# High and low words of a weight tile stored by turns, and weight loads with a stride of two words

## The chip, the cores and the metric

The kernel runs on one core of one Trainium2 chip. The metric is the device time in microseconds (us). Two runs of the kernel before took 2203.51 and 2210.92 us, a median of 2207.22 us.

## What the reference computes

Two stacks of transformer-like blocks work on one sequence: 16 meta tokens and 256 tokens, 1024 features. The first stack has two layers, each a feed-forward part, a mixer (stick-breaking attention beside a convolution of 31 taps) and a second feed-forward part. The second has two layers with differential attention in one and retention in the other, each again between two feed-forward parts. All of it is float32. Nearly all arithmetic is in products of the activations with large weight matrices, of which this is the typical one (2816 hidden features):

```
def swiglu(x, w_gate, w_up, w_down):
    return (jax.nn.silu(x @ w_gate) * (x @ w_up)) @ w_down

for l in range(DEPTH):
    h = h + 0.5 * swiglu(rmsnorm(h, ffn1_norm[l]), ffn1_w_gate[l], ffn1_w_up[l], ffn1_w_down[l])
    h = h + hybrid_mixer(rmsnorm(h, mix_norm[l]), ...)
    h = h + 0.5 * swiglu(rmsnorm(h, ffn2_norm[l]), ffn2_w_gate[l], ffn2_w_up[l], ffn2_w_down[l])
```

## The kernel before, in words

Activations lie with features on the 128 partitions and tokens along the free axis. A **phase** y is one feed-forward part, one mixer, the norm between the stacks, the differential attention or the retention; there are 13, numbered 0 to 12 in the list `PHASES`. Phases 0 to 4 work on all 272 tokens, the later ones on 256 (a mixer's second half already on the narrower set where the next phase is narrow).

**Weights.** SyncE streams 680 panels from memory, each 8 weight tiles of 128x128 (`K8`, 1024 words in a partition) or 11 of them (`K11`, 1408 words), into a ring of four slots, `raw`. TensorE multiplies in a reduced float32 format, so each operand is split into a high part and the rest. For each panel ScalarE writes the rounded high part (`act_split`, L405: `whi` from `raw`), and VectorE the remainder (`dve_split`, L412: `wlo` = `raw` - `whi`). `whi` and `wlo` are two rings of the same form as `raw`, and in each a weight tile is 128 words without a gap.

**Products.** Three matmuls are made for each weight tile k: high weights by high activations, high weights by low activations, low weights by high activations. That is `products` (L387, L388, L389), and `split_products` (L395, L396, L397) where the second goes to another half of the bank. Each matmul comes with a load of its weight tile, 128 words in each partition; the load for the next matmul runs while the present one streams its 272 or 256 activation columns.

**Activations.** The moving operands are in `u` (8 tiles high, 8 tiles low; the input of gate and up or of a mixer's projections), `hid` (22 and 22 tiles; the input of the down projection), in `qk`, `ao_hi` and `ao_lo` (mixers), and in `ry` (retention). `tile_of` gives the address of one: tile k of part 0 (high) or 1 (low), tiles 272 or 256 words apart. In the wide phases the first tile starts at the tensor's start; in the narrow ones it starts `U_PAD` = 112 or `HID_PAD` = 24 words later; `RY_PAD` does the same for `ry`.

**Distances.** With the tensors laid out in the order of the code, each at a multiple of 32 bytes, the start of the moving tile less the start of the weight tile that is loaded beside it comes, modulo 64 words, to this: 48 words in all narrow feed-forward, attention and retention steps; 0, 16, 32 and 48 words by turns in wide steps from `u`; 8, 24, 40 and 56 words by turns in wide steps from `hid` (a moving tile is 272 words further on, a weight tile 128). Within a step the distance is not constant: the moving stream goes through 256 or 272 words while the load goes through 128.

In four panels of eight of each retention head, and in one panel of three of differential attention, the weights are the moving operand and the activations are loaded (L940 to L943, L1049 to L1051).

**Order.** It is written out by hand. SyncE refills a slot of `raw` when VectorE has made the low part; ScalarE writes a slot of `whi` when TensorE has used the panel that was there (`panel_used`); TensorE waits for `lo_ready` at each panel's start, and for a free bank. Between the splits ScalarE and VectorE empty the banks: gates, products with the norm, and the splits of `hid` and `u`.

Of the kernel before, what the change touches and what calls it, by code (L numbers as in the profile page):

```python
# [18 lines left out]
RING = 4  # L19
# [53 lines left out]
def first_col(y):  # L73

    return 0 if y <= LAST_MIX else META
# [68 lines left out]
U_PAD, HID_PAD, RY_PAD = 112, 24, 144  # L144


def build(nc, w8, w11, xT, small, cst, lam, outT):
# [7 lines left out]
    with ctx:  # L155
# [8 lines left out]
        whi = sb("whi", [128, RING, K11], f32r)  # L164
        wlo = sb("wlo", [128, RING, K11], f32r)
# [3 lines left out]
        u = sb("u", [128, 2 * KD * T], f32r)  # L169
# [35 lines left out]
        with ExitStack() as area:  # L205
            hid = sb("hid", [128, 2 * FT * T], f32r, area)
# [158 lines left out]
        def tile_of(buf, tiles, pad, y, part, k, c0, c1):  # L365

            width, first, at = (T, 0, 0) if y <= LAST_MIX else (SEQ, META, pad)
            at += part * tiles * width
            parts = buf[:, at:at + tiles * width].rearrange("p (k c) -> p k c", c=width)
            return parts[:, k, c0 - first:c1 - first]  # L370

        def u_at(y, part, k, c0=None, c1=T):
            return tile_of(u, KD, U_PAD, y, part, k, first_col(y) if c0 is None else c0, c1)

        def hid_at(y, part, f):
            return tile_of(hid, FT, HID_PAD, y, part, f, first_col(y), T)
# [6 lines left out]
        def products(pe, out, slot, k, x_hi, x_lo, first, last):  # L383


            w_h, w_l = whi[:, slot, k * 128:k * 128 + 128], wlo[:, slot, k * 128:k * 128 + 128]
# [4 lines left out]
        def split_products(pe, out, slot, k, x_hi, x_lo, first, last):  # L391


            w_h, w_l = whi[:, slot, k * 128:k * 128 + 128], wlo[:, slot, k * 128:k * 128 + 128]
# [4 lines left out]
        def act_split(act, n, it=0):  # L399

            if not isinstance(it, int) or n < PANELS:
# [211 lines left out]
        def _(pe):  # L613
            def ffn(y):
# [4 lines left out]
                def gate_up(it, norm=False):  # L619

                    for j in range(RING):
# [4 lines left out]
                        for k in range(KD):  # L626
# [5 lines left out]
                            if N == SEQ:  # L632
                                mm = split_products(pe, bank[g % 4], n % RING, k, u_at(uy, 0, k),
                                                 u_at(uy, 1, k), k == 0, k == KD - 1)
                            else:
                                mm = products(pe, bank[g % 4][:, 0:N], n % RING, k, u_at(uy, 0, k),
# [13 lines left out]
            def out_proj(y, n0, per_tile, tiles, x, ready, count, N, lag=3):  # L650
# [4 lines left out]
                def tile(j, it, both):  # L655
                    pe.wait_ge(h_done, KD * (y + 1) + j - 1 + group * it)
                    for q in range(per_tile):
                        n = n0 + per_tile * j + q
                        pe.wait_ge(lo_ready, n + 1 + RING * it)
                        for k in range(tiles):  # L660
# [3 lines left out]
                            if both:  # L664
                                mm = split_products(pe, bank[4 + j % 2], n % RING, k, x(0, K), x(1, K), K == 0, K == last)
# [1685 lines left out]
```

## Time and profile before

| | |
|---|---|
| median of the runs | 2207.22 us |
| the profiled execution: its own time | 2210.91 us |
| its span, first to last instruction | 2209.1 us |
| TensorE matmul busy | 2198.0 us, 18114 matmuls |
| VectorE busy | 1602.4 us |
| ScalarE busy | 1276.6 us |
| GpSimd busy | 282.1 us |
| read from memory | 384.18 MB |

Matmuls are pipelined: each has a duration of about 280 ns in the profile, but the next starts some 115 to 126 ns after it. So what a matmul costs is not its duration but the distance between starts, and that is read by dividing a stretch in which TensorE is never idle by its number of matmuls. Below this is called a **step**.

### The profile page before, as it was taken

The page shows a single profiled execution, that of the slowest core. Times are in us where ns is not written, and L with a number is a line of the kernel's source. Part 1 is how long each engine was busy: PE and PEld are TensorE (multiplying, and loading weights), DVE is VectorE, ACT ScalarE, POOL GpSimd, SP SyncE. Part 2 cuts the span into 40 slices and gives each one's busy share as a digit, 9 for nine tenths or more (in the row PEclk, how much of TensorE's full clock was granted, in tenths as well). Part 3 has the DMA queues.
Part 4 walks back from the last instruction along what each step waited for, and adds up shares of the span by engine and source line. Part 5 has one row for each costly group of instructions (what it writes and reads, how often), then busy time and mean ns, then how long its engine had stood idle before and what let it go on. Part 6 is the DMA issues. An engine that isn't in the chain of part 4 may idle for free.

```text
span 2209.1 us, 48942 instructions
## 1 busy us (share of the span) xinstructions
PE 2198.0 (99%) x18114; PEld 2180.8 (99%) x18114; DVE 1602.4 (73%) x2450; ACT 1276.6 (58%) x1988; POOL 282.1 (13%) x328
## 2 busy tenths in 40 slices
PE   8999999999999999999999999999999999999999
PEld 8999999999999999999999999999999999999999
DVE  6655997665566579887768767888768766777775
ACT  6444786544444368766546646876556645565662
POOL 0001661100100136220020012010010010101000
PEclk9999999999999999999999999999999999999999
DMA  6555435555455544455555555355556645445553
GB/s 229 174 188 165 159 122 170 167 171 195 155 173 183 179 161 144 144 185 186 190 169 193 195 183 163 124 178 194 195 181 200 219 162 177 161 162 194 188 200 124
DMA packets 100408, 386.68 MB, mean 175 GB/s; under 512 B 11312, under 2 KB 12464, under 8 KB 100304
## 3 DMA queue, kind: packets, MB, share of 16 engines
q1 hardware_dynamic: 99648, 383.89, 52.2%
q8 instruction: 68, 1.11, 0.2%
q0 software_dynamic: 368, 1.26, 0.2%
q14 instruction: 36, 0.29, 0.0%
q10 hardware_dynamic: 288, 0.12, 0.0%
HBM read 384.18 MB, written 1.05 MB: 174 GB/s over the span
## 4 chain that ended last, share of the span: by engine, by line
PE 98%; ACT 1%; DVE 1%; issue 0%; DMA 0%; ACTq 0%
PE bank L387 16%; PE bank L389 15%; PE bank L388 15%; PE bank L395 15%; PE bank L396 14%; PE bank L397 14%; PE bank L759 1%; PE bank L1049 1%; PE bank L1050 1%; PE bank L1051 1%; PE bank L1096 0%; PE bank L709 0%; PE bank L740 0%; PE bank L940 0%; PE bank L943 0%; PE bank L942 0%
## 5 line engine op out<-in xcount | busy, mean ns | idle before, releaser
L412 DVE TENSOR_TENSOR wlo<-raw,whi 128x1024 fp32r<-128x1024 f32 (+1 forms) x677 | 893.3, 1322 | 177.8 <-ACT whi L405 165.4
L405 ACT ACTIVATE whi<-raw 128x1024 fp32r<-128x1024 f32 (+1 forms) x677 | 745.5, 1112 | 164.5 <-PE bank L389 117.2
L387 PE MATMUL bank<-u,whi 128*128 128x272 f32 (+1 forms) x1888 | 549.0, 291 | 7.1 <-DVE u L450 7.1
L389 PE MATMUL bank<-u,wlo 128*128 128x272 f32 (+1 forms) x1888 | 543.7, 288 | 0.0
L388 PE MATMUL bank<-u,whi 128*128 128x272 f32 (+1 forms) x1888 | 541.9, 287 | 0.0
L395 PE MATMUL bank<-u,whi 128*128 128x256 f32 x1888 | 529.2, 280 | 0.2
L397 PE MATMUL bank<-u,wlo 128*128 128x256 f32 x1888 | 527.4, 279 | 0.0
L396 PE MATMUL bank<-u,whi 128*128 128x256 f32 x1888 | 527.4, 279 | 0.0
L387 PEld LDWEIGHTS bank<-u,whi 128*128 128x128 f32 x1888 | 356.9, 189 | 8.0 <-DVE wlo L412 7.3
L388 PEld LDWEIGHTS bank<-u,whi 128*128 128x128 f32 x1888 | 357.0, 189 | 0.9 <-issue 0.2
L397 PEld LDWEIGHTS bank<-u,wlo 128*128 128x128 f32 x1888 | 357.6, 189 | 0.0
L395 PEld LDWEIGHTS bank<-u,whi 128*128 128x128 f32 x1888 | 356.4, 189 | 1.0 <-DVE wlo L412 0.5
L389 PEld LDWEIGHTS bank<-u,wlo 128*128 128x128 f32 x1888 | 356.7, 189 | 0.0
L396 PEld LDWEIGHTS bank<-u,whi 128*128 128x128 f32 x1888 | 354.6, 188 | 0.2
L397 PE MATMUL bank<-hid,wlo 128*128 128x256 f32 x770 | 215.0, 279 | 0.0
L395 PE MATMUL bank<-hid,whi 128*128 128x256 f32 x770 | 215.0, 279 | 0.0
L396 PE MATMUL bank<-hid,whi 128*128 128x256 f32 x770 | 215.0, 279 | 0.0
L437 ACT ACTIVATE u<-h,gain 128x256 fp32r<-128x256 f32 (+1 forms) x88 | 44.1, 512 | 280.6 <-DVE h L1650 136.9
L389 PE MATMUL bank<-hid,wlo 128*128 128x272 f32 (+1 forms) x638 | 183.2, 287 | 0.0
L387 PE MATMUL bank<-hid,whi 128*128 128x272 f32 (+1 forms) x638 | 182.9, 287 | 0.0
L388 PE MATMUL bank<-hid,whi 128*128 128x272 f32 (+1 forms) x638 | 182.3, 286 | 0.0
L397 PEld LDWEIGHTS bank<-hid,wlo 128*128 128x128 f32 x770 | 145.9, 190 | 0.0
(332 smaller groups left out, 3448.8 us busy)
## 6 DMA issues: line engine op xcount, KB each, us to landing
raw<-w SPq DMA_DIRECT2D x552, 512.0 KB, 3.4
raw<-w SPq DMA_DIRECT2D x128, 704.0 KB, 4.1
h<-xT SPq DMA_DIRECT2D x4, 272.0 KB, 4.9
outT<-h SPq DMA_DIRECT2D x8, 128.0 KB, 4.7
consts<-cst POOLq DMA_DIRECT2D x1, 576.0 KB, 4.6
dist<-cst POOLq DMA_DIRECT2D x1, 192.0 KB, 2.7
rdist<-cst POOLq DMA_DIRECT2D x1, 192.0 KB, 3.0
sgain<-small POOLq DMA_DIRECT2D x1, 145.5 KB, 4.8
```

The costliest lines, as they stand in the source:

```text
L387: pe.matmul(out, w_h, x_hi, start=first, stop=False)
L388: pe.matmul(out, w_h, x_lo, start=False, stop=False)
L389: return pe.matmul(out, w_l, x_hi, start=False, stop=last)
L395: pe.matmul(out[:, 0:SEQ], w_h, x_hi, start=first, stop=False, skip_group_check=True)
L396: pe.matmul(out[:, SEQ:2 * SEQ], w_h, x_lo, start=False, stop=last, skip_group_check=True)
L397: return pe.matmul(out[:, 0:SEQ], w_l, x_hi, start=False, stop=last, skip_group_check=True)
L405: act.activation(whi[:, n % RING, 0:COLS[n]], raw[:, n % RING, 0:COLS[n]], ACT.Copy).then_inc(hi_ready, 1)
L412: dve.tensor_tensor(wlo[:, n % RING, 0:COLS[n]], raw[:, n % RING, 0:COLS[n]], whi[:, n % RING, 0:COLS[n]], ALU.subtract).then_inc(lo_ready, 1)
L437: act.activation(u_at(y, 0, f), h[:, f, win(y)], ACT.Copy, scale=norm_gain(y, f)).then_inc(u_hi_ready, 1)
L759: mm = pe.matmul(bank[5][:, s0:T], vv[:, i, cols], at[:, hd % 2, c0:c0 + w], start=(i == 0 and n == 0), stop=(i == 2 and n == 2), skip_gro ...
L1049: pe.matmul(bank[2 + i][:, :], u_at(y, 0, k, tok.start, tok.stop), w_h, start=(k == 0), stop=False)
L1050: pe.matmul(bank[2 + i][:, :], u_at(y, 1, k, tok.start, tok.stop), w_h, start=False, stop=False)
```

## The change

The two rings `whi` and `wlo` become one, `whl`, with slots of 2816 words. In it, high and low words of a weight tile stand by turns: word 2c of a tile is the high part of column c, word 2c+1 its low part. `weights(part, n)` gives the view of a panel, [tile, column] with a stride of two words between columns, and ScalarE and VectorE write through this view, VectorE also reads the high part through it. A weight tile then takes 256 words. In the wide phases tiles of the 8-tile panels are laid 272 words apart (`GAP_STEP` = 136 pairs), as the moving tiles are. Panels in which the weights are the moving operand (`STREAMED`) stay as they were, high parts first, low parts after, without stride.

`U_PAD` and `HID_PAD` go. `U_PLACE` and `HID_PLACE` give for each phase the words by which the high tiles are set off from the tensor's start, and the further words by which the low tiles are set off. The tiles of `hid` are 320 words apart in the wide phases. `u` and `hid` become larger by 104 words, and by 2208. `whl` and `u` start at the same place modulo 64 words, and `hid` now too. The numbers in the two tables are therefore the distances, modulo 64 words, between the start of the moving tile and the start of a high weight tile; where a load is of the next tile in a wide 8-tile panel, it is 16 words less. Since the moving stream passes 256 words in the time in which a load passes 128 columns, now 256 words, the distance stays what it is through the whole load.

No instruction is added, removed or moved; splits have the form 128x8x128 in place of 128x1024, and loads a stride of two.

```
-U_PAD, HID_PAD, RY_PAD = 112, 24, 144
+RY_PAD, GAP_STEP, HID_STEP = 40, 136, 320
+U_PLACE = {0: (48, 0), 1: (32, 0), 2: (16, 0), 3: (0, 0), 4: (48, 32), 5: (48, 0), 6: (32, 0), 8: (48, 0), 9: (16, 0), 10: (0, 0), 11: (48, 0), 12: (48, 32), 7: (32, 0)}
+HID_PLACE = {0: (48, 0), 2: (32, 0), 3: (16, 0), 5: (32, 32), 7: (16, 32), 9: (48, 48), 10: (32, 16), 12: (32, 48)}
...
-        whi = sb("whi", [128, RING, K11], f32r)
-        wlo = sb("wlo", [128, RING, K11], f32r)
+        whl = sb("whl", [128, RING, 2 * K11], f32r)
...
-        u = sb("u", [128, 2 * KD * T], f32r)
+        u = sb("u", [128, 2 * KD * T + 104], f32r)
...
-            hid = sb("hid", [128, 2 * FT * T], f32r, area)
+            hid = sb("hid", [128, 2 * FT * HID_STEP + 96], f32r, area)
...
-            width, first, at = (T, 0, 0) if y <= LAST_MIX else (SEQ, META, pad)
-            at += part * tiles * width
-            parts = buf[:, at:at + tiles * width].rearrange("p (k c) -> p k c", c=width)
+            first = first_col(y)
+            at = part * tiles * step + sum(place[:part + 1])
+            parts = buf[:, at:at + tiles * step].rearrange("p (k c) -> p k c", c=step)
             return parts[:, k, c0 - first:c1 - first]
...
+        def weights(part, n):
+            tiles = COLS[n] // 128
+            if n in STREAMED:
+                return whl[:, n % RING, part * K8:part * K8 + K8].rearrange("p (k c) -> p k c", c=128)
+            step = GAP_STEP if n < BASE[LAST_MIX + 1]["P"] and COLS[n] == K8 else 128
+            return whl[:, n % RING, 0:2 * tiles * step].rearrange("p (k c i) -> p k c i", c=step, i=2)[:, :, 0:128, part]
...
-            w_h, w_l = whi[:, slot, k * 128:k * 128 + 128], wlo[:, slot, k * 128:k * 128 + 128]
+            w_h, w_l = weights(0, n)[:, k, :], weights(1, n)[:, k, :]
             pe.matmul(out, w_h, x_hi, start=first, stop=False)
             pe.matmul(out, w_h, x_lo, start=False, stop=False)
             return pe.matmul(out, w_l, x_hi, start=False, stop=last)
...
-                act.activation(whi[:, n % RING, 0:COLS[n]], raw[:, n % RING, 0:COLS[n]],
+                act.activation(weights(0, n), raw[:, n % RING, 0:COLS[n]].rearrange("p (k c) -> p k c", c=128),
                                ACT.Copy).then_inc(hi_ready, 1)
...
-                dve.tensor_tensor(wlo[:, n % RING, 0:COLS[n]], raw[:, n % RING, 0:COLS[n]],
-                                  whi[:, n % RING, 0:COLS[n]], ALU.subtract).then_inc(lo_ready, 1)
+                dve.tensor_tensor(weights(1, n), raw[:, n % RING, 0:COLS[n]].rearrange("p (k c) -> p k c", c=128),
+                                  weights(0, n), ALU.subtract).then_inc(lo_ready, 1)
...
-                        w_h, w_l = (w[:, n % RING, 512 * kk:512 * kk + 512] for w in (whi, wlo))
+                        w_h, w_l = (whl[:, n % RING, K8 * i + 512 * kk:K8 * i + 512 * kk + 512] for i in range(2))
```

## Rows read from the trace of the kernel before

**Rows 1.** Page, part 1: busy time, share of span, instructions.
```profile
PE 2198.0 (99%) x18114; PEld 2180.8 (99%) x18114; DVE 1602.4 (73%) x2450; ACT 1276.6 (58%) x1988; POOL 282.1 (13%) x328
```

**Rows 2.** Waits of TensorE: who waited for whom, us, times, longest.
```profile
PE bank L387 <- DVE u L450: 7.1, 1, 7.1
PE bank L909 <- DVE dn_lo L1966: 0.4, 1, 0.4
```

**Rows 3.** Windows: stretch, length, then busy us (instructions) by engine, clock, DMA share.
```profile
core 0: us, PE busy (x) PEld busy (x) DVE busy (x) ACT busy (x) POOL busy (x), PEclk, DMA share, GB/s
30.00:150.00 120.00, 120.00 (x954) 120.00 (x953) 76.19 (x118) 56.97 (x78) 0.00 (x0) 1.00 0.57 188
520.00:570.00 50.00, 50.00 (x401) 50.00 (x400) 25.57 (x29) 19.27 (x21) 6.30 (x9) 1.00 0.53 175
980.00:1070.00 90.00, 90.00 (x766) 90.00 (x766) 71.35 (x113) 55.61 (x96) 0.00 (x0) 1.00 0.56 187
1450.00:1800.00 350.00, 349.91 (x3080) 349.22 (x3079) 271.24 (x400) 208.37 (x330) 21.75 (x31) 1.00 0.59 195
2030.00:2120.00 90.00, 90.00 (x766) 90.00 (x766) 72.65 (x117) 56.77 (x98) 0.00 (x0) 1.00 0.57 192
830.00:960.00 130.00, 129.84 (x1104) 128.76 (x1103) 118.10 (x198) 103.14 (x182) 56.59 (x59) 1.00 0.45 151
```

**Rows 4.** Groups by line and form: first matmul of each three.
```profile
L395 PE MATMUL bank<-u,whi 128*128 128x256 f32 x1888 | 529.2, 280 | 0.2
L387 PE MATMUL bank<-u,whi 128*128 128x272 f32 x1504 | 439.3, 292 | 7.1 <-DVE u L450 7.1
L395 PE MATMUL bank<-hid,whi 128*128 128x256 f32 x770 | 215.0, 279 | 0.0
L387 PE MATMUL bank<-hid,whi 128*128 128x272 f32 x528 | 152.2, 288 | 0.0
L387 PE MATMUL bank<-u,whi 128*128 128x256 f32 x384 | 109.7, 286 | 0.0
```

**Rows 5.** Timeline of TensorE, wide phase: start, duration.
```profile
502.21 0.29 PE L387 MATMUL bank<-u,whi 128*128 128x272 f32 x1
502.35 0.28 PE L388 MATMUL bank<-u,whi 128*128 128x272 f32 x1
502.46 0.29 PE L389 MATMUL bank<-u,wlo 128*128 128x272 f32 x1
502.59 0.29 PE L387 MATMUL bank<-u,whi 128*128 128x272 f32 x1
```

**Rows 6.** Timeline of TensorE, narrow phase.
```profile
1499.94 0.28 PE L395 MATMUL bank<-u,whi 128*128 128x256 f32 x1
1500.05 0.28 PE L396 MATMUL bank<-u,whi 128*128 128x256 f32 x1
1500.16 0.28 PE L397 MATMUL bank<-u,wlo 128*128 128x256 f32 x1
```

**Rows 7.** Groups by line and form: splits, and VectorE for comparison.
```profile
L412 DVE TENSOR_TENSOR wlo<-raw,whi 128x1024 fp32r<-128x1024 f32 x549 | 686.2, 1252 | 92.5 <-ACT whi L405 80.3
L405 ACT ACTIVATE whi<-raw 128x1024 fp32r<-128x1024 f32 x549 | 574.7, 1052 | 133.1 <-PE bank L389 115.4 <-PE bank L1051 15.4 <-DMA raw<-w 1.8
L1694 DVE TENSOR_TENSOR pr<-sl,up 128x256 f32<-128x256 f32 x110 | 46.8, 426 | 4.7
L1637 DVE TENSOR_REDUCE gt<-bank 128x256 f32<-128x512 f32 x35 | 24.2, 692 | 50.7 <-PE bank L397 50.7
```

More of the change, by code:

```diff
@@ L141 @@
 DA_PANELS = [(part, n) for part, n in DA_PANELS if 0 <= n < DA_HEADS]
-U_PAD, HID_PAD, RY_PAD = 112, 24, 144
+RY_PAD, GAP_STEP, HID_STEP = 40, 136, 320
+U_PLACE = {0: (48, 0), 1: (32, 0), 2: (16, 0), 3: (0, 0), 4: (48, 32), 5: (48, 0), 6: (32, 0), 8: (48, 0), 9: (16, 0), 10: (0, 0), 11: (48, 0), 12: (48, 32), 7: (32, 0)}
+HID_PLACE = {0: (48, 0), 2: (32, 0), 3: (16, 0), 5: (32, 32), 7: (16, 32), 9: (48, 48), 10: (32, 16), 12: (32, 48)}
+STREAMED = {BASE[y]["P"] + j for y, kind in enumerate(PHASES)
+            for j in ([i for i, (part, _) in enumerate(DA_PANELS) if part == 2] if kind == "da" else
+                      [8 * hd + c for hd in range(RT_HEADS) for c in range(4, 8)] if kind == "rt" else [])}
 def build(nc, w8, w11, xT, small, cst, lam, outT):
@@ L389, in products, with split_products @@
             return pe.matmul(out, w_l, x_hi, start=False, stop=last)
-        def split_products(pe, out, slot, k, x_hi, x_lo, first, last):
-            w_h, w_l = whi[:, slot, k * 128:k * 128 + 128], wlo[:, slot, k * 128:k * 128 + 128]
+        def split_products(pe, out, n, k, x_hi, x_lo, first, last):
+            w_h, w_l = weights(0, n)[:, k, :], weights(1, n)[:, k, :]
             pe.matmul(out[:, 0:SEQ], w_h, x_hi, start=first, stop=False, skip_group_check=True)
@@ L816, in out_tile @@
                     for k in range(k0, k1):
-                        mm = products(pe, bank[MIX_OUT[f]][:, 0:N2], (P + 44 + f) % RING, k, qk[:, k, W2], qk[:, KD + k, W2],
+                        mm = products(pe, bank[MIX_OUT[f]][:, 0:N2], P + 44 + f, k, qk[:, k, W2], qk[:, KD + k, W2],
                                       k == 0, k == KD - 1)
@@ L873, in out_tiles @@
                             first = f % 2 == 0 and k == 0
-                            w_h, w_l = (w[:, n % RING, k * 128:k * 128 + 128] for w in (whi, wlo))
+                            w_h, w_l = (weights(i, n)[:, k, :] for i in range(2))
                             for i, (w, x) in enumerate(((w_h, dy_hi), (w_h, dy_lo), (w_l, dy_hi))):
@@ L935, in v_panel @@
                         k = 4 * (p % 2) + kk
-                        w_h, w_l = (w[:, n % RING, 256 * kk:256 * kk + 256] for w in (whi, wlo))
+                        w_h, w_l = (whl[:, n % RING, K8 * i + 256 * kk:K8 * i + 256 * kk + 256] for i in range(2))
                         for i in range(2):
@@ L1025, in da @@
                         cols = slice(k * 128, k * 128 + 128)
-                        w_h, w_l = (own[:, f - RING, cols] if f < RING + OWN else ring[:, n % RING, cols]
-                                    for own, ring in ((dw_hi, whi), (dw_lo, wlo)))
+                        w_h, w_l = (own[:, f - RING, cols] if f < RING + OWN else weights(i, n)[:, k, :]
+                                    for i, own in enumerate((dw_hi, dw_lo)))
                         out = bank[LAST_BANKS[f - RING]][:, 0:SEQ]
```

24 lines of the change are left out of this document (12 added, 12 removed).

## The prediction

> **What bounds the kernel now.** The first view is the page's busy times: TensorE is busy for 2198.0 of 2209.1 us, VectorE for 73%, ScalarE for 58% [rows 1]. The second is the table of TensorE's waits: it has one of 7.1 us at the start and then fractions of a microsecond [rows 2]. So nothing is late for TensorE, and the time is a count of steps times the length of one. The third view, and the one on which all else rests, divides stretches without idle time by their matmuls [rows 3]; the granted clock there is 1.00, the 2.4 GHz level, in each:
> - wide (272 columns), from `u`: 120 us / 954 = 125.8 ns a step; from `hid`: 50 / 401 = 124.7 ns
> - narrow (256 columns): 90 / 766 = 117.5 ns at 980 us and again at 2030 us, but 350 / 3080 = 113.6 ns from 1450 to 1800 us.
>
> At 2.4 GHz, 256 columns are 106.7 ns and 272 are 113.3 ns. A narrow step is 7 to 11 ns above that, a wide one 12.5 ns. Two things speak for the SBUF reads of TensorE itself as the cause. In the narrow phases all distances between stream and load are the same, and all steps nearly so; in the wide ones four distances take turns, and steps differ: the timeline shows 0.14, 0.11 and 0.13 us in a row [rows 5]. And 113.6 and 117.5 ns occur with the same instructions, operand sizes and VectorE share (79% and 77.5%) [rows 3]. What differs there must be how the two streams fall against each other in time, since load and stream pass at different speeds and meet in the course of each step.
>
> The steps at stake: from the counts of the first matmul of each three [rows 4], times three, (1504 + 528) x 3 = 6096 wide ones, and (1888 + 770 + 384) x 3 = 9126 narrow ones. The smaller operands (`qk`, `ao`, `ry`, a narrow remainder of `hid`) add, by the loop counts of the code, some 380 wide and 1050 narrow: 6480 and 10180. I take 3080 of the narrow ones at 113.6 ns and 7100 at 117.5 ns.
>
> **The change, part by part.**
>
> 1. *Stream and load at a constant distance.* The load passes 256 words where it passed 128, as the stream does. Two streams that start apart then stay apart, and if they start on the same place, the one that gives way once is behind for the rest of the load. Before, the load fell back by 128 words against the stream in each step, twice the 64 words after which the pattern of the distances repeats, so there was a meeting in every step. The value of a step without one isn't shown as such. From above it is bounded by today's 125.8 and 117.5 ns; from below by the shortest steps in the timelines, 0.11 us for narrow ones [rows 6], and 6.7 ns more, about 118 ns, for wide ones. I take for narrow steps 113 ns, since a whole stretch ran within 1 ns of it [rows 3]. For wide steps I add to 113 ns what 16 columns cost between 117.5 and 125.8 ns: 121 ns. Then 6480 x (125.6 - 121) = 30 us and 7100 x (117.5 - 113) = 32 us, and 3080 x 0.6 = 2 us: 64 us less.
>
> 2. *Loads with a stride.* No row of before has a load with a stride. The bounds: nothing, as for a load now; and, if the load took twice the time, some 100 ns on each of 16,660 steps, 1.7 ms. I take nothing: the load passes words at the speed at which the moving operand is already read next to it, 256 in 107 ns. It stays in the range with the third rival.
> The Trainium skill has a rule on this (SBUF — State Buffer, the note "SBUF cachelines" in the section on the DMA port swizzle): full bandwidth needs at least two accesses to each line of 16 bytes. A stride of two float32 words gives just two, so by that rule too it costs nothing. No run here shows it yet.
>
> 3. *Splits.* 549 short and 128 long ones on each engine write with a stride, and VectorE reads `whi` with one. Bounds: nothing; twice the time, +1252 ns on VectorE and +1052 on ScalarE for a short one [rows 7]. I take nothing. The nearest row is L1637, which reads a bank with a stride of 256 words: 512 words in 692 ns. The slope between the row of L1694 (256 words, 426 ns) and of L412 (1024 words, 1252 ns) is 1.08 ns a word; L1637 has 266 ns more for 256 words more, 1.04 ns a word, so a stride on the reading side cost it nothing. The cover that VectorE's splits have is thin, though: in narrow gate phases it is busy for 71.35 of 90 us with 32 splits, so 0.58 us could be added to each; in the mixer between 830 and 960 us it is busy for 118.1 of 130 us, and the slack is about 0.3 us for each of 36 or so panels [rows 3]. With steps 4% shorter this slack halves there. I give back 3 us for the two mixers and the attention phase.
>
> 4. *Gaps, pads, the free words behind tensors.* They change no instruction's size: nothing, with no cover needed.
>
> 5. *Streamed weights.* As before, a difference of nothing.
>
> Sum: 2210.9 - 64 + 3 = 2150 us against the profiled execution's own 2210.91 us; that one is 3.7 us above the median shown, which is less than the error of the step lengths, and I leave 2150 us.
>
> **The rivals.**
>
> *The distance doesn't matter, or its good and bad values cancel.* The tables set 0, 16, 32 and 48 words in different phases. In before the wide steps pass through the same four values; if the cost of a step is only that of its distance, each phase now keeps one and the sum over the phases is today's average. For it: the wide average from `hid`, at 8, 24, 40 and 56 words, is within 1.1 ns of that from `u`. Against it: the narrow steps have two lengths at one distance, so the distance isn't all. The time is 2207 us, with some 20 us to each side as some phases do better.
> The Trainium skill says something that ends in the same place (SBUF — State Buffer, "Who interferes with whom": TensorE has a read port for the moving operand and another, independent, for the weights, and never waits on anyone). By it no placement could change a step, and the time would be 2207 us. The trace speaks against the rule as far as the uneven steps go [rows 5], from 0.11 to 0.14 us.
>
> *A constant distance keeps the streams on each other, and the load touches twice as many places for its 128 words.* This ends slower. Each step has now a surplus over its shortest value: 125.6 - 118 = 7.6 ns wide, 117.5 - 111 = 6.5 ns and 113.6 - 111 = 2.6 ns narrow. If an encounter that took part of the step takes all of it, and the surplus doubles everywhere, that adds 6480 x 7.6 + 7100 x 6.5 + 3080 x 2.6 = 49 + 46 + 8 = 103 us: 2310 us. It decides the sign as soon as more steps gain such a surplus than lose it, about half of them; with three in four bad it is near 2260 us. For it: a narrow step has no room, since load and stream are both 107 ns at least.
>
> *VectorE's splits become slow.* At twice the time VectorE's sum is 1602 + 893 = 2495 us, more than TensorE's, and it would set the pace at about 2550 us. It decides from some 0.5 us for a split on.
>
> *All of the surplus goes.* The lower ends: 103 us less, 2107 us.
>
> **How the numbers follow.** I give the forecast 40% (2150 us, its own range 2125 to 2175), no net effect 27% (2185 to 2225), slower by the constant encounter 20% (2240 to 2310), slow splits or slow loads 5%, all of the surplus 8%. A change of 2%, 44 us, is what separates faster and slower from the same, so faster means below 2163 us. Of the forecast's 40% about 35 lie there, with the 8 of the lower end 43. Slower than 2251 us: 5, and most of the 20: 22. The same: 35. The range that leaves out no more than 2 in 10 goes from 2105 to 2280 us.
>
> **What would show it right or wrong.** In the windows of the new profile, a narrow gate phase should have some 796 matmuls in 90 us (113 ns), a wide one 992 in 120 us (121 ns). Phases that differ only in their distance are a test: if the steps of phases 0, 1, 2 and 3 are alike within 1 ns, distance doesn't matter once it's constant; if one is above 130 ns, the second rival holds in it. The splits should stay at 1.25 and 1.05 us; a wait of TensorE for `lo_ready` in the tens of microseconds would mean that they don't. Wrong from the ground up it would be if loads showed another duration than now, or started later after the matmul before.

## The result, and the profile after

The changed kernel takes 2251.55 us (two runs, 2251.3 and 2251.8) against 2207.22 us: slower by a factor of 1.020, with a 95% interval from 1.013 to 1.028. The forecast was 2150 us, a gain.

The page's first line, and TensorE's waits (who waited for whom, us, times, longest), answer to [rows 1, 2]:

```profile
PE 2237.6 (99%) x18114; PEld 2221.3 (99%) x18114; DVE 1603.2 (71%) x2450; ACT 1335.3 (59%) x1988; POOL 284.0 (13%) x328
```
```profile
PE bank L402 <- DVE u L465: 7.5, 1, 7.5
PE bank L924 <- DVE dn_lo L1981: 0.3, 1, 0.3
```

The number of matmuls is the same, no wait has come, and TensorE is busy for 39.6 us more. So the steps themselves became longer. The windows of the profile after (TensorE alone: busy, matmuls, clock, DMA share, GB/s), which answer to [rows 3]:

```profile
30.00:120.00 90.00, 90.00 (x722) 1.00 0.56 181
150.00:200.00 50.00, 50.00 (x393) 1.00 0.46 152
420.00:510.00 90.00, 90.00 (x716) 1.00 0.54 173
610.00:700.00 90.00, 90.00 (x713) 1.00 0.53 172
980.00:1060.00 80.00, 80.00 (x669) 1.00 0.58 190
1170.00:1240.00 70.00, 70.00 (x586) 1.00 0.57 188
1480.00:1540.00 60.00, 60.00 (x503) 1.00 0.62 197
1660.00:1750.00 90.00, 90.00 (x751) 1.00 0.57 184
```

Four of the same windows in the profile before:

```profile
30.00:120.00 90.00, 90.00 (x716) 1.00 0.54 180
150.00:200.00 50.00, 50.00 (x401) 1.00 0.46 156
980.00:1060.00 80.00, 80.00 (x681) 1.00 0.56 190
1660.00:1750.00 90.00, 90.00 (x796) 1.00 0.61 198
```

A window counts the matmuls that its edges cut as well. With two fewer its steps agree with the differences between starts, and I use that from here on: before, narrow steps are then 117.8 ns (80 us / 679) and 113.3 ns (90 us / 794), wide ones from `u` 126.1 ns (90 us / 714). The prediction, which didn't make this correction, has its 117.5 and 125.8 ns 0.3 ns too short and its 124.7 ns 0.6 ns; its 113.6 ns comes from a stretch that also holds the norms' matmuls, and is 0.3 ns too long. Most of this stands on both sides of its subtraction.

After, the four narrow windows, at distances of 48, 32, 16 and 0 words, give 80 / 667 = 119.9, 119.9, 119.8 and 120.2 ns. Four distances, one step: that is the reading that decides. The wide ones from `u` at 48, 16 and 0 words give 125.0, 126.1 and 126.6 ns, and the one from `hid` at 48 words 50 / 391 = 127.9 ns, where it had been 50 / 399 = 125.3 ns.

The groups by line and form show what else changed (busy us, mean ns of one, idle time before), answering to [rows 4, 7]:

```profile
L427 DVE TENSOR_TENSOR whl<-raw,whl 128x1024 fp32r<-128x1024 f32 x549 | 685.8, 1251 | 118.2 <-ACT whl L420 113.6
L420 ACT ACTIVATE whl<-raw 128x1024 fp32r<-128x1024 f32 x549 | 626.0, 1146 | 123.4 <-PE bank L404 106.4 <-PE bank L1066 14.3 <-DMA raw<-w 1.6
...
L404 PEld LDWEIGHTS bank<-u,whl 128*128 128x128 f32 x1888 | 370.3, 196 | 0.0
...
L955 PEld LDWEIGHTS bank<-whl,u 128*128 128x128 f32 x64 | 12.0, 188 | 0.0
```

And the loads of the first matmul of each three in the profile before:

```profile
L387 PEld LDWEIGHTS bank<-u,whi 128*128 128x128 f32 x1888 | 356.9, 189 | 8.0 <-DVE wlo L412 7.3
```

The strided loads last 196 ns. The loads beside the streamed panels (L955), which load activations and have no stride, last 188 ns in the same profile, and in the profile of the kernel before the large groups of loads last 188 to 190 ns. VectorE's split is unchanged (1251 against 1252 ns); ScalarE's, which writes with a stride, went from 1052 to 1146 ns. It is the stride and not the new form that costs: in a run below that keeps the gaps between tiles and drops the stride, it takes 1052 ns again. This cost is covered: VectorE waits 205.7 us for the high part where it waited 165.4 us, and beyond the start (7.7 us of its loads' time, 7.3 before) TensorE waits for neither.

Most of the time is accounted for by the narrow steps: 3080 at 113.3 ns became 120.0 ns, 20.6 us, and 7100 at 117.8 ns became 120.0 ns, 15.6 us; together 36 of the 40.4 us by which the span grew (2249.5 - 2209.1). The wide ones took some of the rest: by their starts, three phases of 528 steps from `hid` give about 2 us, and those from `u` change by about 1 ns or less in both directions. About 2 us are left without an account.

### The profile page after: what moved, and what is told of

It reads as the page before. It is cut to its first block, busy times and chain, and to the rows that moved or that the text cites. A ratio compares the mean times of both kernels' runs of the same rounds, so it can differ in the third digit from the quotient of the medians.

```text
span 2249.5 us, 48980 instructions
## 1 busy us (share of the span) xinstructions
PE 2237.6 (99%) x18114; PEld 2221.3 (99%) x18114; DVE 1603.2 (71%) x2450; ACT 1335.3 (59%) x1988; POOL 284.0 (13%) x328
## 3 DMA queue, kind: packets, MB, share of 16 engines
HBM read 384.18 MB, written 1.05 MB: 171 GB/s over the span
## 4 chain that ended last, share of the span: by engine, by line
PE 97%; ACT 1%; DVE 1%; issue 0%; DMA 0%; ACTq 0%; DVEq 0%
PE bank L402 15%; PE bank L403 15%; PE bank L404 15%; PE bank L410 15%; PE bank L412 15%; PE bank L411 15%; PE bank L774 1%; PE bank L1064 1%; PE bank L1066 1%; PE bank L1065 1%; PE bank L891 1%; ACT whl L420 1%; PE bank L1111 0%; PE bank L724 0%; PE bank L755 0%
## 5 line engine op out<-in xcount | busy, mean ns | idle before, releaser
L427 DVE TENSOR_TENSOR whl<-raw,whl 128x1024 fp32r<-128x1024 f32 (+1 forms) x677 | 893.1, 1321 | 210.7 <-ACT whl L420 205.7
L420 ACT ACTIVATE whl<-raw 128x1024 fp32r<-128x1024 f32 (+1 forms) x677 | 814.3, 1215 | 153.9 <-PE bank L404 107.9
L402 PE MATMUL bank<-u,whl 128*128 128x272 f32 (+1 forms) x1888 | 549.0, 291 | 7.5 <-DVE u L465 7.5
L403 PE MATMUL bank<-u,whl 128*128 128x272 f32 (+1 forms) x1888 | 544.1, 288 | 0.0
L404 PE MATMUL bank<-u,whl 128*128 128x272 f32 (+1 forms) x1888 | 543.1, 288 | 0.0
L410 PE MATMUL bank<-u,whl 128*128 128x256 f32 x1888 | 535.6, 284 | 0.2 <-DVE rqk L2129 0.2
L412 PE MATMUL bank<-u,whl 128*128 128x256 f32 x1888 | 533.2, 282 | 0.0
L411 PE MATMUL bank<-u,whl 128*128 128x256 f32 x1888 | 533.1, 282 | 0.0
L402 PEld LDWEIGHTS bank<-u,whl 128*128 128x128 f32 x1888 | 370.2, 196 | 8.4 <-DVE whl L427 7.7
L403 PEld LDWEIGHTS bank<-u,whl 128*128 128x128 f32 x1888 | 370.3, 196 | 0.8 <-issue 0.2
L404 PEld LDWEIGHTS bank<-u,whl 128*128 128x128 f32 x1888 | 370.3, 196 | 0.0
L410 PEld LDWEIGHTS bank<-u,whl 128*128 128x128 f32 x1888 | 368.6, 195 | 0.8 <-DVE whl L427 0.3
L412 PEld LDWEIGHTS bank<-u,whl 128*128 128x128 f32 x1888 | 369.0, 195 | 0.0
L411 PEld LDWEIGHTS bank<-u,whl 128*128 128x128 f32 x1888 | 368.6, 195 | 0.2
L412 PE MATMUL bank<-hid,whl 128*128 128x256 f32 x770 | 218.7, 284 | 0.0
L410 PE MATMUL bank<-hid,whl 128*128 128x256 f32 x770 | 217.7, 283 | 0.0
L411 PE MATMUL bank<-hid,whl 128*128 128x256 f32 x770 | 217.0, 282 | 0.0
L404 PE MATMUL bank<-hid,whl 128*128 128x272 f32 (+1 forms) x638 | 184.3, 289 | 0.0
L402 PE MATMUL bank<-hid,whl 128*128 128x272 f32 (+1 forms) x638 | 184.3, 289 | 0.0
L403 PE MATMUL bank<-hid,whl 128*128 128x272 f32 (+1 forms) x638 | 183.5, 288 | 0.0
L411 PEld LDWEIGHTS bank<-hid,whl 128*128 128x128 f32 x770 | 150.8, 196 | 0.0
```

The lines of the kernel that those rows point to most:

```text
L402: pe.matmul(out, w_h, x_hi, start=first, stop=False)
L403: pe.matmul(out, w_h, x_lo, start=False, stop=False)
L404: return pe.matmul(out, w_l, x_hi, start=False, stop=last)
L410: pe.matmul(out[:, 0:SEQ], w_h, x_hi, start=first, stop=False, skip_group_check=True)
L411: pe.matmul(out[:, SEQ:2 * SEQ], w_h, x_lo, start=False, stop=last, skip_group_check=True)
L412: return pe.matmul(out[:, 0:SEQ], w_l, x_hi, start=False, stop=last, skip_group_check=True)
```

## The experiments

Two theories were set against each other. **A**: the load with a stride is itself longer, and a narrow step, in which the load has no room, is set by it. **B**: the constant distance keeps stream and load in each other's way. Later two more came up, on why contiguous narrow steps have two lengths.

### Steps alone

Only TensorE works, on data already in place; nothing of the reference is computed. Each line repeats one kind of step 48 times:

```
w[:, 128 * k:128 * k + 128]                                                 # stride 1
w[:, 256 * k:256 * (k + 1)].rearrange("p (c i) -> p c i", i=2)[:, :, 0]     # stride 2
for i in range(n): mm = pe.matmul(bank[i % 2][:, 0:256], W(i % 8, 2), X(i % 8, 256, 16), start=True, stop=True)
```

> Only matmuls, 48 in a row of each kind, in a program that computes nothing of the reference: 16, 256, 272 or 512 moving columns, loads with a stride of 1, 2 or 4 words, start distances of 0 to 56 words. Theory A (a strided load is itself longer): with 16 moving columns, where only the load can set the step, about 111 ns at stride 1 and about 119 ns at stride 2, whatever the distance; narrow steps at stride 2 then 119 to 120 ns at every distance, wide ones hardly above those at stride 1. Theory B (the two streams get in each other's way at a constant distance): with 16 columns both strides 111 ns, and at 256 columns stride 2 differs by 5 ns or more between distances. A stride of 4 words: by A at least 119 ns, by B as stride 2.

Measured from the starts of the matmuls, once the first eight of a line are past: narrow at stride 2, at 0, 16, 32 and 48 words: 120.0, 120.0, 121.1 and 120.1 ns. Narrow at stride 1: 157 ns in the line at 0 words, during which the clock changed, 117.8 at 16, 118.7 at 32, 113.3 at 48. Wide at stride 1: 125.3, 126.7, 126.6, 123.3 ns; at stride 2: 124.5, 125.9, 124.5, 127.6 ns. The contiguous narrow lines were repeated at the end of the program: 120.0, 117.8, 120.0 and 117.8 ns at 0, 16, 32 and 48 words. At 32 and at 48 words the same instructions thus gave two lengths.

The lines with 16 columns settle only half of the question. In the first one, with contiguous loads, 43 steps took 111.7 ns at a granted clock of 1.00; then, with TensorE streaming only 16 columns a step, the granted clock fell to its 1.2 GHz level (0.50). The lines with stride 2 and 4 ran wholly at that level, and it rose again in the lines of narrow steps behind. At the 1.2 GHz level a step took 213.3 ns with a contiguous load and with one of stride 2 alike, and 233.3 ns with stride 4. What remained open was the strided load by itself at the 2.4 GHz level.

Two other lines gave large numbers, the first a load with a stride of four words and the second a moving operand with a stride of two (query by source line: durations, first and last start, form):

```profile
L74 PE MATMUL bank<-x,w x48: 389/396/397, 151.8 to 162.8; 128*128 128x256 f32 x48
```
```profile
L75 PE MATMUL bank<-x,w x48: 388/409/417, 163.0 to 173.8; 128*128 128x256 f32 x48
```

11.0 / 47 = 234 ns and 10.8 / 47 = 230 ns a step, at a granted clock of 1.00.

### The places alone

The two contiguous rings of before, with the tables and tile distances of the change:

```
-U_PAD, HID_PAD, RY_PAD = 112, 24, 144
+RY_PAD, GAP_STEP, HID_STEP = 40, 136, 320
+U_PLACE = {0: (48, 0), 1: (32, 0), 2: (16, 0), ...}
+HID_PLACE = {0: (48, 0), 2: (32, 0), ...}
```

> The kernel before with its two contiguous weight rings, and with the change's tables of places and tile distances for u, hid and ry. Theory A (the stride in the load costs the time): narrow steps go back to 113 to 118 ns, load duration 188 ns, time 2190 to 2215 us. Theory B (the places cost it): narrow steps near 120 ns, time 2240 to 2255 us.

2227.13 us, 1.008 of before (1.006 to 1.011). Neither range held it: slower than A allowed, much faster than B. Its windows:

```profile
150.00:200.00 50.00, 50.00 (x408) 1.00 0.47 160
...
980.00:1060.00 80.00, 80.00 (x682) 1.00 0.54 189
1170.00:1240.00 70.00, 70.00 (x592) 1.00 0.57 196
1480.00:1540.00 60.00, 60.00 (x511) 1.00 0.54 187
1660.00:1750.00 90.00, 90.00 (x753) 1.00 0.56 192
```

So places do matter where loads are contiguous: 48 words 117.6, 32 words 118.6, 16 words 117.9, 0 words 119.8 ns in the narrow windows. The first row is wide steps from `hid`, whose distance is now constant at 48 words: 50 / 406 = 123.2 ns against 125.3 before. Of the 40 us that the change costs, the span of this run (2225.3 us) takes 16; the stride on top of the same places, 24. The 16 us are not a cost that places add to the strided kernel, in which four places give one step. They come for the most part from phases 9 and 10, which ran at 113.3 ns at 48 words and now run at 117.8 to 120.0 ns at others.

### The stride with one place

```
-U_PLACE = {0: (48, 0), 1: (32, 0), 2: (16, 0), ...}
-HID_PLACE = {0: (48, 0), 2: (32, 0), 3: (16, 0), ...}
+U_PLACE = {y: (48, 0) for y in range(13)}
+HID_PLACE = {y: (48, 0) for y in range(13)}
```

> The changed kernel with one distance, 48 words, in all phases. Theory A: narrow steps stay at 120.0 ns, load duration 196 ns, 2245 to 2255 us. Theory B: as narrow phases with 48 words cost what they cost now, and others follow them; if 0, 16 or 32 words were the bad ones the time falls by 10 us or more.

2248.78 us, 1.018 of before (1.014 to 1.021), as by A. The narrow windows are again 120 ns each, now all at 48 words:

```profile
980.00:1060.00 80.00, 80.00 (x669) 1.00 0.54 187
1170.00:1240.00 70.00, 70.00 (x586) 1.00 0.57 195
1480.00:1540.00 60.00, 60.00 (x502) 1.00 0.57 193
1660.00:1750.00 90.00, 90.00 (x750) 1.00 0.54 186
```

### A grid of places, and the load by itself

Again only TensorE, in the kernel's order of three, with 36 steps a line; nothing of the reference is computed. To keep the clock up, the load by itself is measured beside 128 columns, half of a narrow step's.

```
def triple(pe, N, sw, wstep, xstep, p0, p1, k): ...   # views: weights with stride sw, tiles wstep apart; moving tiles xstep apart, at p0, low ones p1 further
for i in range(12): ... pe.matmul(out, w_h, x_h); pe.matmul(out, w_h, x_l); pe.matmul(out, w_l, x_h)
```

> Only matmuls, in the kernel's order of three (high by high, high by low, low by high), twelve times each, in a program that computes nothing of the reference. Contiguous loads with start distances of the high tile from 0 to 56 words and of the low tile 0 to 56 words further, narrow (twice, in opposite order) and wide (weight tiles 144 apart with moving tiles 272 apart; 128 with 320; 128 with 272); loads of stride 2 at 16 and 8 pairs; and 128 and 192 columns at both strides. Theory A (the strided load itself takes longer): 128 and 192 columns, where the load sets the step, about 111 to 113 ns at stride 1 and 119 to 120 ns at stride 2; narrow steps at stride 2 never below 119.5 ns on average; contiguous ones between 113 and 120 ns. Theory B (meetings at a constant distance): 128 columns alike at both strides.

The loads of the two lines with 128 columns, first stride 1, then stride 2:

```profile
L354 PEld LDWEIGHTS bank<-x,w x36: 190/192/192, 1342.4 to 1346.3; 128*128 128x128 f32 x36
```
```profile
L355 PEld LDWEIGHTS bank<-x,w x36: 197/198/199, 1346.4 to 1350.6; 128*128 128x128 f32 x36
```

3.9 us / 35 = 111 ns and 4.2 / 35 = 120 ns; from the starts of the matmuls, 111.8 and 120.0 ns. This is theory A shown directly: with half of the columns gone, a strided load still holds the step at the length that the narrow windows of the changed kernel have. All eight narrow lines at stride 2 gave 119.2 to 121.0 ns. The length isn't quite a constant: beside 192 columns the strided load makes a step of 118.3 ns, below the 119 that was expected, where the contiguous one makes 111.7; and over whole phases the narrow steps from `hid` in the changed kernel are 120.0 ns three times, 119.4 and 120.4 ns.

The contiguous narrow lines, 64 places twice, gave 116.5 to 121.5 ns, with one exception: the high tile at 48 words and the low one likewise. It gave 113.3 ns in the first pass and 117.8 ns in the second:

```profile
L103 PE MATMUL bank<-x,w x36: 276/276/286, 233.4 to 237.4; 128*128 128x256 f32 x36
```
```profile
L134 PE MATMUL bank<-x,w x36: 281/281/283, 365.1 to 369.2; 128*128 128x256 f32 x36
```

So 48 words, where the kernel before already had its narrow phases, is the only place with a step of 113.3 ns, and even there it isn't certain. It isn't the only place with two lengths: the high tile at 32 words and the low one 16 further gave 117.8 ns in the first pass and 121.5 in the second, 0 and 8 words 120.1 and 117.1 ns. For wide steps the grid had 122.8 ns at 40 words and 124.3 at 48 words, both with weight tiles 144 and moving tiles 272 words apart, and 123.3 ns at 48 words with 128 and 320. Over all 64 places, wide steps with tiles at a constant distance of their starts (144 and 272) ranged from 122.8 to 127.2 ns; the 16 lines with a changing distance (128 and 272) gave 124.6 to 126.3 ns. A constant distance is thus no gain as such: it depends on the place.

Within each kernel and each program here the weight tiles of narrow steps start at one place modulo 64 words, and only the moving tiles are shifted. So the rows of one run can't tell a distance between the two from a place of the moving tile alone. What speaks for the distance is that, by the order and sizes of the tensors, everything in the grid lies 32 words further on than in the kernels, modulo 64, and 48 words has the same two lengths in both.

### Stride undone in the panels of 11 tiles

```
             tiles = COLS[n] // 128
...
+            if COLS[n] == K11:
+                return whl[:, n % RING, part * K11:part * K11 + K11].rearrange("p (k c) -> p k c", c=128)
```

> The changed kernel with the stride undone in the panels of 11 tiles alone (down projections), all places as in the change. Theory A: narrow steps from hid go from 120.0 ns to what the run with contiguous rings and these places had there, 117 to 120 ns, load duration 188 ns there; steps from u stay at 120.0 ns with 196 ns; wide steps from hid 123 to 127 ns; together about 7 us less, 2242 us. Theory B: no step changes by more than 1 ns.

2245.88 us, 1.017 of before (1.013 to 1.020), 5.7 us below the change where about 7 were expected. Loads from `hid` are back at 188 to 189 ns. The starts give narrow steps from `hid` of 119.9, 117.8, 118.7, 121.1 and 117.0 ns in the five phases; four are near the lengths that they had with contiguous rings, one, expected at 118, is 121. The first wide one is 126.7 ns, not 123.3, at the same constant 48 words. And phase 7's steps from `u`, whose loads weren't touched, went from 120.0 to 121.1 ns. So the loads and most steps did what was expected of them, and on top of the stride there is a second cause of 1 to 3 ns that depends on more than the place.

### Contiguous, with constant distances

If the stride is the cost and the constant distance a gain, the two can be had apart: leave weights contiguous, and make tile distances agree modulo 64 words by gaps. Only the starts then keep their distance; within a step the stream still passes 256 words while the load passes 128.

```
-RY_PAD, GAP_STEP, HID_STEP = 40, 136, 320
+RY_PAD, GAP_STEP, HID_STEP = 40, 144, 320
-            return whl[:, n % RING, 0:2 * tiles * step].rearrange("p (k c i) -> p k c i", c=step, i=2)[:, :, 0:128, part]
+            return whl[:, n % RING, part * K11:part * K11 + tiles * step].rearrange("p (k c) -> p k c", c=step)[:, :, 0:128]
```

with all places at (48, 0).

> Contiguous weights (high and low parts apart in each slot), with tiles 144 words apart in the wide 8-tile panels and moving tiles 272 apart in u, 320 in hid: the start distance is 48 words in all phases, 32 for the load of the next wide tile. Theory A: no load costs more than before; wide steps from hid 123.3 ns as in the run with contiguous rings, where 48 words stood in the first phase, against 124.7 to 125.3 before; wide steps from u 123.5 to 126 ns; narrow ones 113.5 or 117.8 ns as before. 2190 to 2210 us, at or below the kernel before. Theory B: above 2230 us, since distances are constant here too.

2192.12 us, 0.993 of before (0.990 to 0.996): the first version that beats both. It differs from the run with the stride and one place only in the stride and in the gap that goes with it, and is 57 us faster.

```profile
30.00:120.00 90.00, 90.00 (x727) 1.00 0.56 180
150.00:200.00 50.00, 50.00 (x408) 1.00 0.49 157
...
980.00:1060.00 80.00, 80.00 (x681) 1.00 0.56 187
1170.00:1240.00 70.00, 70.00 (x596) 1.00 0.61 194
1480.00:1540.00 60.00, 60.00 (x531) 1.00 0.59 192
1660.00:1750.00 90.00, 90.00 (x797) 1.00 0.64 201
```

Wide steps from `u` are 90 / 725 = 124.1 ns (126.1 before), from `hid` 123.2 ns (125.3). Narrow ones are 117.8 in two windows and 113.3 in two, as before; nothing changed in their distances.

### One disturbance

Only TensorE again; nothing of the reference is computed. Theory C is that a stream has two ways to run and a single disturbance chooses, theory D that something outside TensorE sets the step. Most narrow streams at 48 words follow six triples at 56 words and one extra matmul, six follow triples at 56 words or other places without one, and twelve follow an extra matmul in a running stream:

```
for i in range(6): ...     # at 56 words
pe.matmul(bank[1][:, 0:96], w[:, 0:128], x[:, 48:144], start=True, stop=True)
for i in range(16): ...    # at 48 words
```

> Only matmuls, in a program that computes nothing of the reference: narrow contiguous steps at 48 words, which ran at 113.3 ns in one place and at 117.8 ns in another, each time after six triples at 56 words and one extra matmul of 16 to 512 columns or at another distance; and such extra matmuls put into a running stream at 48 words. Theory C (two stable ways in which stream and load fall against each other, and a single disturbance chooses): some extra matmuls lead to 113.3 ns and others to 117.8 ns, each value holding over all 48 steps. Theory D (something outside TensorE sets the step): all sections alike, since nothing else runs here.

Each of the 40 streams settled on 113.3 or on 117.8 ns, none between. Four of them, after 96 and 128 columns from the lead at 56 words, and with 64 and then 96 columns in a running stream:

```profile
L68 PE MATMUL bank<-x,w x48: 281/281/347, 60.2 to 65.8; 128*128 128x256 f32 x48
```
```profile
L71 PE MATMUL bank<-x,w x48: 276/276/333, 68.1 to 73.5; 128*128 128x256 f32 x48
```
```profile
L138 PE MATMUL bank<-x,w x48: 276/276/365, 256.2 to 261.7; 128*128 128x256 f32 x48
```
```profile
L140 PE MATMUL bank<-x,w x48: 281/281/347, 261.8 to 267.4; 128*128 128x256 f32 x48
```

The median duration tells the two ways apart, 276 and 281 ns. With no other engine at work both exist, an extra matmul can lead from either to the other, and theory D falls. Not every one does: in the running stream, those of 32, 192, 224, 272 and 320 columns came on a stream at 117.8 ns and left it there. And the six streams that followed other triples without an extra matmul all ran at 113.3 ns.

### 40 words in the wide phases

```
-U_PLACE = {y: (48, 0) for y in range(13)}
+U_PLACE = {y: (40, 0) if y < 5 else (48, 0) for y in range(13)}
```

> The contiguous version with gaps of 16 words, now with 40 words in place of 48 in the wide phases for u, which gave 122.8 against 124.3 ns in the grid of start distances. If the grid's values hold in the kernel: 4500 wide steps from u 1.5 ns shorter, 7 us less than the version with 48 words, about 2185 us. If neighbouring engines or loops decide instead: 124 to 126 ns and 2190 to 2200 us.

A miss: 2208.93 us, 0.997 of before (0.994 to 1.000). The wide steps from `u` were 125.0 ns (90 us / 720 in the window from 30 us), not 122.8. The grid's value, from 36 steps in a row, did not carry over to the kernel; why isn't shown. Phases 9 and 10 ran at 117.8 ns in this profile (90 us / 765 in the window from 1660 us), which is about 14 of the 16.5 us between its span and that of the version with 48 words.

### An extra matmul in each narrow feed-forward phase

```
+                            if N == SEQ and norm and j == 1 and k == 0:
+                                pe.matmul(bank[g % 4][:, 0:128], weights(0, n)[:, 0, :], u_at(uy, 0, 0, META, META + 128),
+                                          start=True, stop=True, skip_group_check=True)
```

The next matmul overwrites the result. One run with 64 columns, one with 128.

> The contiguous version with gaps, with one more matmul of 64 columns in each narrow feed-forward phase, after the norm's matmul and ahead of the second panel (its result is overwritten). In the matmul-only run such a matmul took a stream from 117.8 to 113.3 ns. If the way in which stream and load fall against each other is chosen by one disturbance and then held, narrow phases that ran at 117.8 ns in the run without it now run at 113.3 ns from that point on: up to 30 us less, 2160 to 2175 us. If it is chosen anew by something else, run times stay at the levels of the version without it, 2191 or 2199 us.

> As the run with 64 columns, with 128, which also took a stream from 117.8 to 113.3 ns in the matmul-only run. Same two outcomes; if the length of the extra matmul matters in the kernel as it did there with 96 and 160 columns, which kept 117.8 ns, the two runs may differ by multiples of about 7 us, one phase each.

With 64 columns 2185.81 us, 0.990 of before (0.986 to 0.993); with 128 columns 2181.87 us, 0.987 (0.982 to 0.991), the fastest kernel here. The windows of the latter:

```profile
980.00:1060.00 80.00, 80.00 (x709) 1.00 0.59 192
1170.00:1240.00 70.00, 70.00 (x597) 1.00 0.59 191
...
2060.00:2130.00 70.00, 70.00 (x620) 1.00 0.64 206
```

Phases 5 and 12, at 117.8 ns without it, now run at 113.2 and 113.3 ns; phase 7, between them, runs at 117.6. That is less gain than the 2160 to 2175 us that were expected if all phases followed. Nor did phase 7 simply stay as it was. In its timeline the first panel, before the norm, still runs at the short step (1135.24 to 1137.85 us, 23 steps of 113 ns), and the long one begins behind the norm and the extra matmul (1139.59 to 1142.42 us, 24 steps of 118 ns):

```profile
1135.24 0.28 PE L410 MATMUL bank<-u,whl 128*128 128x256 f32 x1
...
1137.85 0.28 PE L412 MATMUL bank<-u,whl 128*128 128x256 f32 x1
...
1139.18 0.41 PE L648 MATMUL bank<-u,whl 128*128 128x128 f32 x1
...
1139.59 0.28 PE L411 MATMUL bank<-u,whl 128*128 128x256 f32 x1
...
1142.42 0.28 PE L411 MATMUL bank<-u,whl 128*128 128x256 f32 x1
```

### A second one in phase 7

```
-                            if N == SEQ and norm and j == 1 and k == 0:
+                            if N == SEQ and norm and k == 0 and j in ((1, 2) if y == FINAL + 1 else (1,)):
```

> The version with an extra matmul of 128 columns, and in phase 7, the one narrow feed-forward phase that stayed at 117.8 ns, a second one ahead of the third panel. If a stream at 117.8 ns goes to 113.3 ns by such a matmul, as in the matmul-only run, phase 7's 1580 steps lose 4.4 ns each: 7 us less, 2171 to 2178 us. If what comes before phase 7 fixes it in another way, no change: 2178 and 2185 us as before.

2186.24 us, 0.990 of before (0.985 to 0.995): no gain. The timeline of phase 7 (start, duration) tells what the second one did. The first extra matmul (L648) comes at 1139.02 us, the second at 1142.04 us:

```profile
1139.02 0.41 PE L648 MATMUL bank<-u,whl 128*128 128x128 f32 x1
...
1140.12 0.28 PE L411 MATMUL bank<-u,whl 128*128 128x256 f32 x1
...
1141.93 0.28 PE L412 MATMUL bank<-u,whl 128*128 128x256 f32 x1
1142.04 0.22 PE L648 MATMUL bank<-u,whl 128*128 128x128 f32 x1
...
1142.27 0.28 PE L411 MATMUL bank<-u,whl 128*128 128x256 f32 x1
...
1144.04 0.28 PE L411 MATMUL bank<-u,whl 128*128 128x256 f32 x1
```

Between the two, 16 steps take 1.81 us, 113 ns each; behind the second, 15 take 1.77 us, 118 ns. In this execution the stream ran at 113 ns before the norm and again behind the first extra matmul, where the same instructions had left 118 ns in the profile of the run before; the second led out of the short way. So an extra matmul doesn't select a way: one of 128 columns has now been followed by a change in either direction and by none. Phase 9 ran at 117.6 ns in this profile (60 us / 510 in the window from 1480 us) with the same one extra matmul with which it had run at 113.4; that alone is the 7 us by which this execution is longer than the one profiled there.

## Why the prediction was wrong, by its steps

**Loads with a stride** is the step that failed: "I take nothing: the load passes words at the speed at which the moving operand is already read next to it". Its own upper bound of 100 ns was far off, but the value isn't zero. Beside 128 columns a step goes from 111.8 to 120.0 ns by the stride of the load alone (in the grid), and in the kernel the load is 196 ns long instead of 188. The prediction had named just that as a sign of being wrong from the ground up. A narrow step can't hide it, since without the stride it was 113.3 or 117.8 ns, below the 120.0 of the strided load. That makes 2.2 ns where a step was 117.8 and 6.7 ns where it was 113.3, in all 36 us. A wide step can in part: from `u` at 48 words it is 125.0 ns with the stride and 124.1 in the contiguous version with gaps; from `hid`, with the same places and tile distances, 127.9 ns with the stride against 123.2 with contiguous rings, though 126.7 in the run in which the stride was undone there.

The argument from the moving operand was faulty in a way that the trace could have shown. The moving operand is contiguous. That a contiguous stream passes its words at some speed says nothing of one that takes every second word, and for the moving operand itself a stride of two nearly doubles the step, to 230 ns.

The rule that was weighed there (the Trainium skill, SBUF — State Buffer, the note "SBUF cachelines": two accesses to a line of 16 bytes are enough for full bandwidth) gave the same zero. By this case it holds neither for the load, 8.2 ns longer, nor for the moving operand, which also makes two accesses to a line. At a stride of four words, one access to a line, the step is 234 ns. So its direction is borne out, its threshold is not.

**Stream and load at a constant distance**: forecast 113 ns narrow, 121 ns wide, 64 us. Nothing of it came: with the stride, narrow steps are 120 ns and wide ones 125.0 to 127.9 ns. Whether the two streams then keep their distance all through a step, as was assumed, no run shows. With contiguous weights, constant distances of the starts, all at 48 words, are worth 2.0 ns a wide step from `u` and 2.1 from `hid` (126.1 to 124.1, 125.3 to 123.2), about 13 us where 30 were forecast, and by the grid that is a matter of the place as much as of the constancy; for narrow steps they are worth nothing, since 113.3 ns isn't the value of a constant distance but one of two ways at one distance. To take a stretch at 113.6 ns as what all narrow steps would reach was the second error, of 32 us: the term of 7100 steps was sized at 4.5 ns a step, and no run gave any of it by a change of distances. It was at hand: the distance was the same in both stretches, as the prediction itself says, so a change of distances could not be what separates them. One of the two grounds for the mechanism was also misread: the unequal steps of 0.14, 0.11 and 0.13 us [rows 5] are differences of starts rounded to 10 ns; by the starts to the nanosecond they are 130, 120 and 123 ns, uneven still, but by 10 ns and not by 30.

**The splits**: taken as nothing, and nothing on VectorE (1251 ns). ScalarE's took 94 ns more, against the sign that they would stay at 1.05 us, which its slack covers: it was busy for 58% of the span. The 3 us given back for the mixers can't be told apart in the result.

**Gaps and pads** added no cost that a run shows; **streamed weights** kept their 188 ns loads.

**The rivals.** The outcome, 2251.55 us, lies within the range that was given (2105 to 2280), by the range's width and not by the forecast, at the lower edge of the case that ends slower. That case's mechanism was half right: "the load touches twice as many places for its 128 words". Its other half, that the distances decide, was wrong: 0, 16, 32 and 48 words all give 120 ns. The rival that the distance doesn't matter was right for strided narrow steps, and not for contiguous ones, and its time, 2207 us, left out the stride. The prediction's own test, whether phases 0 to 3 are alike within 1 ns, came out between the two rivals: 125.0, 126.1 and 126.6 ns in phases 0, 2 and 3, and none above 130. The rule of the Trainium skill named there (SBUF — State Buffer, "Who interferes with whom": two independent read ports, TensorE waits on no one) doesn't agree with these runs. In a program in which nothing else works, contiguous narrow steps range from 113.3 to 121.5 ns with the place of the moving tiles, and by two independent ports I would expect one number. The place isn't all of it, though, since single places have two lengths.

The sign was wrong because the two largest terms, 30 and 32 us of gain, stood against a zero with a bound of 1.7 ms. A value between such ends was chosen without a row near it.

What stays open is why a strided load takes longer, and what makes a contiguous stream settle on one length or the other, at 48 words above all. No run separates the causes inside TensorE's reads. That placements repeat after 64 words was assumed; what speaks for it is that narrow tiles 112 words into `u` in the kernel before and 48 words in the contiguous version have the same two lengths, 113.3 and 117.8 ns.

## What to carry to other kernels

Where moving columns and load take nearly the same time (256 columns make a step of 113.3 ns at least, a contiguous load of 128 one of 111.8), there is no room for a slower load, and a few nanoseconds count in each of ten thousand steps; an operand's stride has to be measured alone, beside few columns, before a layout is built on it. Read the step from the starts, and compare it between stretches with the same instructions: two lengths at one address pattern mean that a part of the time is not set by the layout, and a forecast shouldn't book it. If an idea has two parts, here the stride and the constant distance, look for the form that has only the one: contiguous weights with gaps of 16 words, all at one good place, had a gain of 0.7% without the cost.

## What else the runs showed

- Run times of the kernel before come in levels. In the comparison beside the run with 40 words, its 17 runs are 2203.5 to 2204.4 (7), 2210.7 to 2211.8 (5), 2217.1 and 2218.0, and 2224.5 to 2224.9 us (3). A narrow feed-forward phase has 44 x 24 + 16 x 33 = 1584 steps, and 1584 x 4.5 ns = 7.1 us: each level fits one more phase at 117.8 in place of 113.3 ns. The run with 128 columns has levels too, 2178.5, 2178.7 and 2185.1, 2185.4 us. That the levels are phases is worked out, and shown phase by phase only in the profiled executions.
- A load with a stride of four words and a moving operand with a stride of two words make a step of 234 and 230 ns, against 113 to 120 ns contiguous.
- ScalarE writes with a stride of two words 9% slower (1146 against 1052 ns for 1024 words). VectorE, which reads and writes with it, takes the same time (1251 and 1252 ns).
- With a stride of two words the cost of the load shows at the 2.4 GHz level and not at the 1.2 GHz level. There, beside 16 columns, a step is 213.3 ns with a contiguous load and with a stride of two; with a stride of four words it is 233.3 ns, the same as beside 256 columns at the 2.4 GHz level.
